# Depthwise convolution of a conformer block: taps moved from TensorE and VectorE to GpSimd in five of eight channel blocks

## The reference, cut to what matters

```python
def conformer_conv(h, w_pw1, b_pw1, w_dw, b_dw, ln_g, ln_b, w_pw2, b_pw2):
    a = h @ w_pw1 + b_pw1
    u = a[..., :D_MODEL] * jax.nn.sigmoid(a[..., D_MODEL:])
    u = lax.conv_general_dilated(u, w_dw[:, None, :], window_strides=(1,),
                                 padding=[(CONV_WIDTH - 1, 0)],
                                 feature_group_count=D_MODEL) + b_dw      # 31 taps, each channel by itself
    mu = mean(u); var = mean(square(u - mu))
    u = (u - mu) * rsqrt(var + EPS) * ln_g + ln_b
    return silu(u) @ w_pw2 + b_pw2
```

## Time and profile before

| | us |
|---|---|
| median of 3 runs (2295.31 to 2297.5) | 2295.83 |
| the profiled execution, its time | 2295.76 |
| its span in the profile | 2294.0 |
| stage of the convolution in that span, first `u` to end of `conv(7)` | 630.08 to 739.85 |

### The profile page before, as it was taken

The page is one execution under the profiler, slowest core; times in us unless marked ns, Lnnn a source line. Parts: engine busy times, 40 slices in busy tenths (PEclk is TensorE's granted clock), DMA queues, the critical chain, the costliest instruction groups (busy, mean ns, idle before and its releaser), DMA issues.

```text
span 2294.0 us, 29956 instructions
## 1 busy us (share of the span) xinstructions
PE 2279.8 (99%) x11025; PEld 1853.9 (81%) x11025; DVE 1291.8 (56%) x1740; ACT 826.9 (36%) x1158; POOL 103.1 (4%) x98
## 2 busy tenths in 40 slices
PE   9999999999999999999999999999999999999999
PEld 8877888888865788888887777888889889888888
DVE  5454643444598654444548878554456756654553
ACT  5376532322413532322434555222224223422222
POOL 0000000000000000000004311000001001000003
PEclk9999999999999999999999999999999999999999
DMA  5210322222463232222331112332222322323221
GB/s 200 83 46 28 116 95 101 92 100 92 174 172 108 74 101 97 96 101 92 101 110 66 54 48 73 120 100 93 101 92 72 115 99 74 111 93 100 101 92 56
DMA packets 65947, 220.05 MB, mean 96 GB/s; under 512 B 8704, under 2 KB 11136, under 8 KB 65600
## 3 DMA queue, kind: packets, MB, share of 16 engines
q1 hardware_dynamic: 65568, 218.49, 28.7%
q10 hardware_dynamic: 288, 0.30, 0.0%
HBM read 208.56 MB, written 2.10 MB: 92 GB/s over the span
## 4 chain that ended last, share of the span: by engine, by line
PE 92%; DVE 4%; ACT 2%; issue 1%; DMA 0%; POOL 0%; DVEq 0%; ACTq 0%; SPq 0%; POOLq 0%
PE ps L1973 85%; PE ps L2469 2%; PE ps L2563 1%; PE ps L2589 1%; DVE wlo L1007 1%; PE ps L2332 1%; ACT whi L403 0%; PE ps L2579 0%; PE ps L2347 0%; PE ps L2596 0%; PE ps L2312 0%; DVE acc L1035 0%; ACT sl L610 0%; ACT sph L619 0%; ACT sl L605 0%
## 5 line engine op out<-in xcount | busy, mean ns | idle before, releaser
L1973 PE MATMUL ps<-xh,whi 128*128 128x512 f32 (+1 forms) x1832 | 708.6, 387 | 2.5 <-DVE wlo L1208 1.4
L1973 PE MATMUL ps<-xh,wlo 128*128 128x512 f32 (+1 forms) x1832 | 699.9, 382 | 0.0
L1973 PE MATMUL ps<-xl,whi 128*128 128x512 f32 (+1 forms) x1832 | 699.5, 382 | 0.0
L1007 DVE TENSOR_TENSOR wlo<-raw,whi 128x1024 fp32r<-128x1024 f32 x380 | 471.7, 1242 | 222.0 <-ACT whi L403 212.6
L403 ACT ACTIVATE whi<-raw 128x1024 fp32r<-128x1024 f32 x380 | 398.4, 1050 | 468.4 <-PE ps L1973 466.8
L1973 PE MATMUL ps<-yh,whi 128*128 128x512 f32 (+1 forms) x1196 | 451.8, 378 | 0.6 <-DVE yl L1780 0.5
L1973 PE MATMUL ps<-yh,wlo 128*128 128x512 f32 (+1 forms) x1196 | 448.5, 375 | 0.0
L1973 PE MATMUL ps<-yl,whi 128*128 128x512 f32 (+1 forms) x1196 | 448.4, 375 | 0.0
L1973 PEld LDWEIGHTS ps<-xh,whi 128*128 128x128 f32 x1832 | 344.7, 188 | 76.3 <-issue 6.5
L1973 PEld LDWEIGHTS ps<-xl,whi 128*128 128x128 f32 x1832 | 344.6, 188 | 68.3 <-issue 3.1
L1973 PEld LDWEIGHTS ps<-xh,wlo 128*128 128x128 f32 x1832 | 344.4, 188 | 67.1
(11 more groups left out here) (307 smaller groups left out, 1834.4 us busy)
## 6 DMA issues: line engine op xcount, KB each, us to landing
raw<-stream SPq DMA_DIRECT2D x380, 512.0 KB, 3.2
u<-ub SPq DMA_DIRECT2D x118, 67.0 KB, 2.1
tapw<-taps SPq DMA_DIRECT2D x1, 3584.0 KB, 11.3
h<-x_t SPq DMA_DIRECT2D x8, 256.0 KB, 5.8
out_t<-h SPq DMA_DIRECT2D x16, 128.0 KB, 1.7
raw<-stream SPq DMA_DIRECT2D x7, 256.0 KB, 6.5
const<-consts SPq DMA_DIRECT2D x1, 1025.0 KB, 9.1
raw<-stream ACTq DMA_DIRECT2D x1, 256.0 KB, 3.8
```

The lines of the kernel that those rows point to most:

```text
L1007: dve.tensor_tensor(wlo[:, a.slot], raw[:, a.slot], whi[:, a.slot].bitcast(F32), ALU.subtract)\
L1973: mm = pe.matmul(out, lhs, rhs, start=first and n == 0, stop=last and n == 2, skip_group_check=skip)
```

## The change

In blocks 0 to 4 TensorE makes four groups (16 taps) where it made five (20). GpSimd makes five taps: a product into `cv`, then four times a product into `lnb` and an addition of `lnb` to `cv`, nine instructions, each waiting for the one before. VectorE's ten taps follow: its first one waits for all nine of GpSimd's instructions and is a multiply-add onto `cv`, where it was a plain product. Blocks 5 to 7 stay as they are. Cut to its core:

```diff
-GROUPS = (5, 5, 5, 5, 5, 5, 7, 7)
+GROUPS = (4, 4, 4, 4, 4, 5, 7, 7)
-OWN_AT = tuple(sum(OWN[:b]) for b in range(len(OWN) + 1))
+CENTERED = 5
+POOL_TAPS = tuple(5 if b < CENTERED else 0 for b in range(len(OWN)))
+POOL_AT = tuple(sum(max(2 * n - 1, 0) for n in POOL_TAPS[:b]) for b in range(len(OWN) + 1))
+DVE_TAPS = tuple(OWN[b] - POOL_TAPS[b] for b in range(len(OWN)))
+OWN_AT = tuple(sum(DVE_TAPS[:b]) for b in range(len(OWN) + 1))
...
             act.wait_ge(rrow_ready, SUM["lnvar"])
+            act.wait_ge(s("cv_pool"), POOL_AT[KB])
...
-                for n in range(n0, min(n1, OWN[b])):
-                    k, cvb = TAPS - OWN[b] + n, A["cv"][:, b]
+                for n in range(n0, min(n1, DVE_TAPS[b])):
+                    k, cvb = TAPS - DVE_TAPS[b] + n, A["cv"][:, b]
                     u, tap = A["ub"][:, b % 2, k:k + T], col("w_dw", b * TAPS + k)
-                    if n == 0:
+                    if n == 0 and POOL_TAPS[b]:
+                        dve.wait_ge(s("cv_pool"), POOL_AT[b + 1])
+                        op = dve.scalar_tensor_tensor(cvb, u, tap, cvb, ALU.mult, ALU.add)
+                    elif n == 0:
                         dve.wait_ge(s("pw_u"), b + 1)
-                        if b < CENTERED:
-                            op = dve.tensor_scalar(cvb, u, tap, None, ALU.mult)
...
+            def pool_taps(b):
+
+                for n in range(POOL_TAPS[b]):
+                    k, cvb = TAPS - OWN[b] + n, A["cv"][:, b]
+                    u, tap = A["ub"][:, b % 2, k:k + T], col("w_dw", b * TAPS + k)
+                    if n == 0:
+                        pool.wait_ge(s("pw_u"), b + 1)
+                        pool.wait_ge(rrow_ready, SUM["pw"] + 1)
+                        pool.tensor_scalar(cvb, u, tap, None, ALU.mult).then_inc(s("cv_pool"), 1)
+                    else:
+                        pool.wait_ge(s("cv_pool"), POOL_AT[b] + 2 * n - 1)
+                        pool.tensor_scalar(lnb[:], u, tap, None, ALU.mult).then_inc(s("cv_pool"), 1)
+                        pool.wait_ge(s("cv_pool"), POOL_AT[b] + 2 * n)
+                        pool.tensor_tensor(cvb, cvb, lnb[:], ALU.add).then_inc(s("cv_pool"), 1)
+
+            for b in range(KB):
+                pool_taps(b)
```

More of the change, by code:

```diff
@@ L50 @@
 PIVOT = 2
-CENTERED = 5
 FF_GROUPS = (8, 8, 6)
@@ L264, in build @@
                   "v_half sb_o sb_yh sb_yl wo_early wo_added "
-                  "taps_in u4_in0 u4_in1 u4_in2 pw_t1 pw_t2 pw_sg pw_u pad_zero u4_act u4_pool cv_pe cv_chain cv_done piv_ready cen_ready cen_sq "
+                  "taps_in u4_in0 u4_in1 u4_in2 pw_t1 pw_t2 pw_sg pw_u pad_zero u4_act cv_pe cv_pool cv_chain cv_done piv_ready cen_ready cen_sq "
                   "ln_s1 ln_acc mean_mm mean_sq ln_var cen_again ln_t ln_s "
@@ L1463, in own_taps @@
             def own_taps(b, n0, n1):
-                for n in range(n0, min(n1, OWN[b])):
-                    k, cvb = TAPS - OWN[b] + n, A["cv"][:, b]
+                for n in range(n0, min(n1, DVE_TAPS[b])):
+                    k, cvb = TAPS - DVE_TAPS[b] + n, A["cv"][:, b]
                     u, tap = A["ub"][:, b % 2, k:k + T], col("w_dw", b * TAPS + k)
-                    if n == 0:
+                    if n == 0 and POOL_TAPS[b]:
+                        dve.wait_ge(s("cv_pool"), POOL_AT[b + 1])
+                        op = dve.scalar_tensor_tensor(cvb, u, tap, cvb, ALU.mult, ALU.add)
+                    elif n == 0:
                         dve.wait_ge(s("pw_u"), b + 1)
-                        if b < CENTERED:
-                            op = dve.tensor_scalar(cvb, u, tap, None, ALU.mult)
-                        else:
-                            dve.wait_ge(s("piv_ready"), 2)
-                            op = dve.scalar_tensor_tensor(cvb, u, tap, A["mu"][:], ALU.mult, ALU.add)
+                        dve.wait_ge(s("piv_ready"), 2)
+                        op = dve.scalar_tensor_tensor(cvb, u, tap, A["mu"][:], ALU.mult, ALU.add)
                     else:
@@ L1882, in _ @@
                 pool.tensor_copy(A["u4"][32 * d:32 * d + 32, (KB - 1) % 3, i],
-                                 A["ub"][32 * i:32 * i + 32, (KB - 1) % 2, d:d + COPY]).then_inc(s("u4_pool"), 1)
+                                 A["ub"][32 * i:32 * i + 32, (KB - 1) % 2, d:d + COPY]).then_inc(s("cv_pool"), 1)
             def stage(pair, e):
@@ L2461, in conv @@
                     pe.wait_ge(s("u4_act"), LAST_ACT)
-                    pe.wait_ge(s("u4_pool"), SHIFTS * 4 - LAST_SP - LAST_ACT)
+                    pe.wait_ge(s("cv_pool"), POOL_AT[KB] + SHIFTS * 4 - LAST_SP - LAST_ACT)
                 if b >= 2 + CENTERED:
```

## The result

The changed kernel takes 2332.45 us in the median of 6 runs (2332.05 to 2334.33), the kernel before 2295.86 on the same chip: a ratio of 1.0159, with a 95% interval of 1.0149 to 1.0170. It is 36.6 us slower. The span of the profiled execution is 2330.8 us, 36.8 more than before, and nearly all of that arises between the first and the last end of `gated`.

A forecast was written before the change was run, and what follows sets the result against it. TensorE was taken as the bound, VectorE nearly as full; u(5) 25.5 us late, less 0.8 regained and 1.3 spare, moves the end by 23.4: 2295.76 + 23.4 = 2319.2 us, range 2302 to 2333.

The forecast's parts named there:

- The loop: GpSimd's nine, VectorE's first tap, then the next `gated`, on which GpSimd waits: 18.4 us per block, first 16.8.
- TS: GpSimd's product with a weight per partition, five per block: taken as 0.70 us, bounds 0.61 and 1.09.
- The second rival: GpSimd's product with a weight costs as much as a two-input product, 1.09 us: 2329 us in all, chance 0.17.
- TT: GpSimd's addition in place of two tensors, four per block: 1.29 us each.
- The turns: GpSimd and VectorE instructions reading SBUF, VectorE's with two inputs there, go one after the other, each its length less 0.14 us.
- u(b): Time at which `gated` ends on VectorE for block b; u(5) was forecast at 720.9 us, 25.5 later than before.
- VectorE's part: From GpSimd's end to the next end of `gated`: notice, four multiply-adds, `take_gate` to `gated`, `gated` itself; together 5.3 us.
- `pivot_sum`: VectorE's operation that takes one turn with GpSimd, once in the five rounds: 0.4 us.
- The clock: TensorE idle before `conv(6)` might run it at the lower level: 0 to +4.2 us, taken as 0.
- TensorE's waits: In the changed profile TensorE was to wait before `conv(1)` to `conv(6)`, some 10.7 us before `conv(6)`.
- The signs to look for: Steps of about 18 us; L1477 well over 751 ns in blocks 0 to 4; first-tap waits a little over 1 us.
- The forecast of the gain: Five groups taken from TensorE at 0.89 us each, 4.4 us the most that the change can give.

The follow-up runs named there:

- e3_memset: Changed kernel with GpSimd's taps replaced by thirteen chained memsets per block, which read nothing; VectorE's first tap, a plain product, waits for the last: 2319.84 us, 1.0104.
- e6_pe20: Changed kernel, but TensorE keeps 20 taps in blocks 0 to 4, so VectorE has six instead of ten; GpSimd's five stay: 2326.38 us, 1.0132.
- e1_order: Changed kernel with all ten of VectorE's taps moved behind the next `gated`, same instructions: 2317.94 us, 1.0095.
- e7_unwaited: Kernel before, plus GpSimd's nine instructions per block into buffers no one reads; TensorE 20 taps, VectorE 11: 2313.73 us, 1.0077.
- e4_two_input: Changed kernel with GpSimd's products made as two-tensor products, the weight broadcast along the row: 2325.86 us, 1.013.
- e8_clock: Changed kernel with 28 spare products on TensorE before `conv(6)`, so that it does not stand idle: 2332.12 us, 1.0161.
- e9_free: Changed kernel with GpSimd's five taps left out and nothing in their place; TensorE 16 taps, VectorE ten: 2292.03 us, 0.9984.
- e2_apart: Changed kernel with GpSimd summing in its own buffer; VectorE starts with its own product and adds that sum after its tenth tap: 2312.72 us, 1.0072.

## Why the prediction was right, and where it was not

**The direction and its place.** The loop was named, and it is what happened: e3_memset shows it costing 24.0 us with no reads shared, e6_pe20 shows that VectorE's load does not set it, and e1_order gets 14.5 us back by order alone. Second, e7_unwaited shows sharing as a price of its own, 17.9 us. The two don't add up (24.0 + 17.9 against 36.6): in the ring VectorE stands still for part of GpSimd's time and is held up less, with a mean of 848 ns for its multiply-adds against 1005 in e7_unwaited (751 before). The change's own trace says how much of each there is. Its first step, in which hardly anything runs beside the nine, is the bare ring of 19.1 us; five of those are 95.6 of the 103.0 us. So the ring makes some 30 of the 37.6 us by which the five steps grew, and what the engines take from each other in the later four the other 7.4.

**The term that was mis-sized: the product on GpSimd (TS).** It was put at 0.70, with bounds of 0.61 and 1.09; it measures 1.57 with nothing beside it. The prediction reasoned that one tensor input makes it like the copy. It costs more than the product of two tensors, 1.04 in e4_two_input. Five per block are 4.4 us a loop. The second rival, a TS of 1.09, was the right idea and still fell short.

**What made up for part of it.** The pause between chained instructions is 0.09 us, not 0.14. With the TT at 1.30, the nine alone take 5 x 1.57 + 4 x 1.30 + 8 x 0.09 = 13.8, where 9.9 was predicted. The turns were over-priced: 3.2 us in a later loop, measured 15.6 - 13.75 = 1.85. Turns as the prediction has them, up to 0.14 us before the other's end, hold beside an addition and not beside a product with a weight. A split begun 0.10 us into an addition (677.31) took 2.27, its own 1.22 and 1.05 of the 1.20 that the addition had left; one begun 0.10 into a product (669.86) took 1.67, with only 0.45 of 1.47. It is the same with multiply-adds. The one that began 0.40 us into the addition at 673.73 was held up to 0.20 before the end of that:

```profile
674.13 1.66 DVE L1481 SCALAR_TENSOR_TENSOR cv<-ub,vec,cv 128x512 f32<-128x512 f32 x1
```

The other four of its five, begun beside products, took 0.74 to 1.06. The five took 5.34 us instead of 3.9, where one for one with additions and products of the measured lengths they would have taken 5 x 0.61 + 3 x 1.15 + 2 x 1.43 = 9.4. So the nine end 15.7 us after u(b) in a later loop, where 13.1 was predicted: 2.6 too short, four times, and 2.35 in the first (13.85 for 11.5).

The section Who interferes with whom of SBUF — State Buffer in the Trainium skill, which the prediction cites, gives its rule for two inputs in SBUF without an operation (a list behind it names `tensor_tensor`). L1477 does contend, as that rule has it. That the second instruction blocks for the whole of the other agrees with the traces beside an addition, to within 0.20 us, and does not beside a product with a weight; there the measurement decides.

**VectorE's part** was put at 5.3 and is 5.26 (first loop: 643.53 to 648.79). `pivot_sum` was given 0.4 and shows nothing: its round, the fourth, is the shortest of the later four (20.90). u(0) itself is 0.4 earlier. u(5) therefore comes at 732.66 instead of 720.9, 11.8 us later than predicted.

**Behind the loop.** The steps from u(5) to u(7) give back 0.8 as predicted (31.07 against 31.86). `conv(6)` begins at 761.17, which is u(6) + 13.4 exactly. The 1.3 us that were spare between `conv(6)` and the landing of block 7 did not come through: from u(7) to the end of `conv(7)` it is 12.50, before 12.56. These terms give 11.8 + 1.2 = 13.0, nearly the whole difference of 13.3 between 2332.45 and 2319.2.

**The clock** was left at 0 from a range up to +4.2. TensorE's timeline of the change has the wait:

```profile
761.17 15.06 PE L2491 MATMUL ps<-u,tapw 128*32 128x512 f32 x112 [7.92 <-DMA u<-ub]
```

After 7.92 us of idleness the granted clock is 0.50, the 1.2 GHz level, from 761.00 to 765.70. The row that the choice of 0 rested on, a clock of 1.00 in every window of before, comes from a trace whose longest wait of TensorE is 1.5 us. It says nothing of a wait of 7.92, so the choice had no row for it. `conv(7)` was ready at about u(7) + 5.2 = 768.9 and began at about 770.0, since `conv(6)` was late; that is most of the missing 1.2, and e8_clock gets about one us of it back in the trace.

**TensorE's waits** were expected at `conv(1)` to `conv(6)`. Only two are at a `conv`; the longest, 20.9 us, is at the pivot's product after tile 9, L2504, for VectorE's `pivot_sum` (L1494), which is queued behind the late taps. It costs nothing of its own: VectorE, which makes the steps, waits for no product of TensorE between u(0) and u(7), and TensorE still has the 7.92 us before `conv(6)` to spare.

**The signs to look for.** The prediction called itself wrong if TS left 0.61 to 1.09, and by that sign this step is wrong. L1477 "well over" 751 in blocks 0 to 4 holds only in part: the mean is 848 ns, as the first five taps of each block run after GpSimd has stopped. The other five, in blocks 0 to 3, take 1.04 in the mean. VectorE's wait at a first tap was 4.4 to 10.3, not a little over 1. The range's top end, 2333, was made of a TS of 1.09 and a `conv(6)` wholly at the lower clock; the time lies beside it for another reason, the longer TS. With a TS outside its bounds and turns too dear, it was partly luck that the time stayed inside the range.

**The forecast of the gain.** Five groups on TensorE at 0.89 are 4.4 us at most, as predicted; e9_free shows 3.8 in the medians and 4.3 in the stage. What the change moves was never worth more.

**Open.** Why GpSimd's product with a weight per partition is slower than one with two tensors, and why it holds VectorE up less than an addition does, isn't settled by these runs; they measure it only.

## What to carry to other kernels

When work goes to another engine, draw the ring of waits first: a chain that starts at an engine's own output and must end before that engine's next one sets a least length for every round, however idle either engine is (18.2 us in e3_memset, with VectorE busy for 11.4). Place the consumer a full round later, and then price both engines anew with the sharing between them, since that becomes the next bound. Take the length of an instruction only from rows of that very form; the product with a weight was not between the copy and the two-tensor product but above both.

## What the runs showed of the hardware

- GpSimd's product of 128x512 f32 with a weight per partition takes 1.57 us alone, 1.89 to 1.93 in the mean of a block's later four where VectorE has ten or eleven taps, and 2.63 at most (e2_apart and e7_unwaited). The two-tensor product takes 1.04, an addition 1.29, a memset of 128x1024 0.955. The Trainium skill, GPSIMD Engine Reference, section Engine selection, calls operations with one input roughly line-rate; the copy at 0.62 comes near to that, with 0.48 for VectorE's own product with one input; the product with a weight, at 1.57, does not, and the measurement decides.
- Sharing also lengthens VectorE's plain product with one input in SBUF, from 0.48 to 0.91 us beside GpSimd (e7_unwaited). A VectorE instruction whose input is in PSUM keeps 0.69.
- How long GpSimd holds up a VectorE instruction with two inputs in SBUF depends on GpSimd's instruction. Beside an addition or a product of two tensors such an instruction that begins second gets going 0.14 to 0.20 us before the other's end (a split of 2.27 instead of 1.22 in the change, one of 2.01 in e4_two_input). A split begun 0.10 us into a product with a weight loses only 0.45 us of the 1.47 that are left (1.67 instead of 1.22), though that product is the longest of the three.
- TensorE's clock was 0.50 for the first 4.5 us of work after a wait of 7.92 us, and 1.00 in the same place when spare products filled all but 1.92 us of the wait.
